# A two-layer hybrid encoder step: up-projection of the gated feed-forward by seven block products per tile pair, down-projection as a phase of its own

## The reference, cut to what matters

```
def conv_ffn(h, w_in, conv_w, conv_b, w_out, pad):
    T = h.shape[1]
    u = h @ w_in                      # 1024 -> 2 * 2816
    up = jnp.concatenate([pad.astype(u.dtype), u], axis=1)
    c = conv_b + sum(up[:, j:j + T] * conv_w[j] for j in range(CONV_W))
    g, val = jnp.split(c, 2, axis=-1)
    y = (jax.nn.silu(g) * val) @ w_out
    return y, up[:, up.shape[1] - (CONV_W - 1):]
```

## Time and profile before

| | |
|---|---|
| median of three runs | 3229.93 us (3226.78 to 3233.74) |
| profiled execution | span 3231.0 us from first to last instruction; of its own time no other figure is given |
| TensorE, matmuls | 3061.2 us busy, 95% of the span |
| VectorE | 2022.1 us, 63% |
| ScalarE | 1139.7 us, 35% |
| GpSimd | 984.7 us, 30% |
| granted TensorE clock, mean | 0.983 of full |
| first feed-forward | about 702 to 1490 us of the span |
| second feed-forward | about 2251 to 3039 us |

### The profile page before, as it was taken

The page is one execution under the profiler, slowest core; times in us unless marked ns, Lnnn a source line. Parts: engine busy times, 40 slices in busy tenths (PEclk is TensorE's granted clock), DMA queues, the critical chain, the costliest instruction groups (busy, mean ns, idle before and its releaser), DMA issues.

```text
span 3231.0 us, 50014 instructions
## 1 busy us (share of the span) xinstructions
PE 3061.2 (95%) x18949; PEld 2945.9 (91%) x18949; DVE 2022.1 (63%) x3233; ACT 1139.7 (35%) x2398; POOL 984.7 (30%) x591
## 2 busy tenths in 40 slices
PE   7999999899999999998987999999999999999998
PEld 6888888799999999998977888889999999999997
DVE  6666666347666556667776677762766666555765
ACT  4555555223221222223340666651322222222243
POOL 2222222222222212222324677753222221222231
PEclk9999999899999999999988999999999999999999
DMA  5222222311111111111104121221111111111111
GB/s 114 70 69 72 67 68 89 106 40 43 44 46 46 42 44 45 41 45 55 40 25 125 31 59 51 83 94 46 40 46 47 46 40 46 46 40 46 55 40 62
DMA packets 255742, 181.94 MB, mean 56 GB/s; under 512 B 26981, under 2 KB 238645, under 8 KB 255541
## 3 DMA queue, kind: packets, MB, share of 16 engines
q1 hardware_dynamic: 240728, 165.11, 17.9%
q10 hardware_dynamic: 14812, 13.97, 1.4%
HBM read 142.54 MB, written 36.50 MB: 55 GB/s over the span
## 4 chain that ended last, share of the span: by engine, by line
PE 76%; DVE 11%; issue 6%; ACT 5%; POOL 1%; DMA 1%; ACTq 0%; DVEq 0%; SPq 0%; POOLq 0%
PE ps L963 22%; PE ps L965 21%; PE ps L964 21%; PE ps L1146 2%; ACT t L1662 2%; PE ps L1281 2%; PE ps L1099 2%; PE ps L1082 2%; PE ps L1166 1%; DVE t L2170 1%; DVE t L2093 1%; DVE ps L2085 1%; DVE t L2020 1%; ACT t L1718 1%; PE ps L1261 1%
## 5 line engine op out<-in xcount | busy, mean ns | idle before, releaser
L963 PE MATMUL ps<-t,t 128*128 128x384 f32 (+1 forms) x4920 | 1648.7, 335 | 52.7 <-issue 10.6
L965 PE MATMUL ps<-t,t 128*128 128x384 f32 (+1 forms) x4920 | 1616.1, 328 | 0.0
L964 PE MATMUL ps<-t,t 128*128 128x384 f32 (+1 forms) x4920 | 1614.5, 328 | 0.0
L963 PEld LDWEIGHTS ps<-t,t 128*128 128x128 f32 x4920 | 931.4, 189 | 91.0 <-issue 24.1
L964 PEld LDWEIGHTS ps<-t,t 128*128 128x128 f32 x4920 | 932.1, 189 | 1.2 <-issue 0.5
L965 PEld LDWEIGHTS ps<-t,t 128*128 128x128 f32 x4920 | 930.7, 189 | 0.0
L780 POOL TENSOR_TENSOR t<-t,t 128x1024 fp32r<-128x1024 f32 x181 | 471.2, 2603 | 1238.9 <-ACT t L1549 1235.5
L1979 DVE TENSOR_TENSOR t<-t,ps 128x384 f32<-128x384 f32 x528 | 260.0, 523 | 147.1 <-PE ps L965 145.0
L1549 ACT ACTIVATE t<-t 128x1024 fp32r<-128x1024 f32 x130 | 138.0, 1061 | 413.8 <-PE ps L965 413.8
L2265 DVE TENSOR_SCALAR t<-t 128x2 f32 (+1 forms) x88 | 14.7, 167 | 419.7 <-ACT t L1792 419.7
L1780 ACT ACTIVATE t<-ps 128x384 f32<-128x384 f32 x176 | 86.4, 494 | 470.1 <-PE ps L965 470.1
(11 more groups left out here) (168 smaller groups left out, 3316.3 us busy)
## 6 DMA issues: line engine op xcount, KB each, us to landing
t<-in_w_ffn_in SPq DMA_DIRECT2D x88, 512.0 KB, 3.7
t<-in_w_ffn_out SPq DMA_DIRECT2D x44, 512.0 KB, 3.2
t<-in_w_qkv_a SPq DMA_DIRECT2D x24, 512.0 KB, 3.8
t<-in_w_ple_gate SPq DMA_DIRECT2D x16, 512.0 KB, 3.5
out<-t SPq DMA_DIRECT2D x32, 192.0 KB, 2.1
t<-in_w_o_a SPq DMA_DIRECT2D x8, 512.0 KB, 3.7
t<-in_w_q_b SPq DMA_DIRECT2D x8, 512.0 KB, 4.2
t<-in_w_o_b SPq DMA_DIRECT2D x8, 512.0 KB, 3.7
```

What stands on the lines that cost most here:

```text
L963: pe.matmul(out, a_hi, b_hi, start=start, stop=False, skip_group_check=True)
L964: pe.matmul(out, a_hi, b_lo, start=False, stop=False, skip_group_check=True)
L965: return pe.matmul(out, a_lo, b_hi, start=False, stop=stop, skip_group_check=True)
```

## The change: what it does, and the diff

The first two tile pairs of a layer are made as before. The other 20 (PAIRS) take block products. The up-projection of a pair is seen as a 2 x 2 block product. A11 and A12 are the gate tile's weights for the first and the second half of k (4 k-tiles x 128 outputs each), A21 and A22 the value tile's. The activations are the two halves of k by the first two segments. Seven products of 4 k-tiles at 384 columns replace eight; the third segment of 320 columns stays a plain product of four blocks.

- Weights: SP loads the four blocks (256 KB each) of the next pair as soon as the product that used the old block is done (blk_done 1, 3, 6, 8). GpSimd makes S1 to S4 from them (four instructions of 512 columns) and the rest of all eight (`block_rest`); ScalarE rounds all eight. Each of the eight has one slot.
- Activations: three combined operands t_hi/t_lo (4 k-tiles x 384) and a fourth, kept in DRAM and then laid over the first half of h's second segment (t4). They are made once per layer at its entry: VectorE makes four parts of 384 columns for each of four k-tiles from x (`combined_parts`), GpSimd combines them (`combine`, four instructions for each k-tile), ScalarE rounds, and VectorE subtracts (`combined_low`).
- Sums: ScalarE copies the first product out; VectorE makes five sums of 384 columns, each with one input from PSUM (u2, u3, and three into ubuf). TensorE accumulates A12's product on the first bank, and S4's on the bank of S1 once VectorE has read it (sums_made 3).
- Filter and gate have the same instructions as before, in the order of `pair` and `gate_half` on VectorE.
- A gated tile (ffr, 557 KB) goes to DRAM (`store_tile`). When the pairs are done the tiles come back four at a time (`load_tiles`), are rounded by ScalarE into h_hi and subtracted by VectorE into h_lo (`tile_high`, `tile_low`).
- Down-projection: six blocks, five of four tiles and one of two, 24 jobs each; a job sums over 4 k-tiles. There are 144 adds per layer instead of 264, in eight banks (JOB_BANKS), in the last block five.

The core of the diff (indentation of 12 columns taken off where a line has it; "..." marks what is left out):

```diff
+PAIRS = NFF - 2
+F_ADDS = 6
+F_CHUNKS, F_JOBS = 4 + 4 * 5 + 2, 8 + 4 * 5 * 5 + 22
+U_KEPT = 12 + 3 * PAIRS
+JOB_BANKS = (7, 1, 2, 4, 6, 5, 0, 3)
+LAST_BANKS = (7, 4, 6, 5, 3)
...
+    def load_block(name, n):
+        q, k0 = divmod("A11 A12 A21 A22".split().index(name), 2)
+        n0 = DFF * q + P * (2 + n)
+        sp.dma_start(slots[l][name][2].rearrange("p (k n) -> p k n", n=P),
+                     w_ffn_in[l].rearrange("(k p) n -> p k n", p=P)[:, 4 * k0:4 * k0 + 4, n0:n0 + P]
+                     ).then_inc(blk_loaded[name], 16)
+    def store_tile(t):
+        sp.wait_ge(ff_made, f0 + t + 1)
+        sp.dma_start(ff_dram[:, t, :], ffr[:, 0:T]).then_inc(ff_stored, 16)
+    def load_tiles(j):
+        for k in range(4 if j < 5 else 2):
+            sp.dma_start(ff_raw[j % 2][:, k, :], ff_dram[:, 4 * j + k, :]).then_inc(ff_loaded[j % 2][k], 16)
+    def down_chunk(j, h):
+        c = c0 + 4 + 4 * j + h
+        if j < 5:
+            load_chunk(c, 0, 0, w_raw[c % 2][:, :].rearrange("p (k n) -> p k n", n=256),
+                       w_ffn_out[l].rearrange("(k p) n -> p k n", p=P)[:, 4 * j:4 * j + 4, 256 * h:256 * h + 256])
...
+    sp.wait_ge(chunk_done, c0 + 3)
+    load_block("A11", 0)
+    load_block("A21", 0)
+    sp.wait_ge(comb_made, COMB_MADE + 16 * (l + 1))
+    load_block("A22", 0)
...
+    sp.wait_ge(chunk_done, c0 + 4)
+    load_block("A12", 0)
+    for n in range(PAIRS):
+        done = 8 * (PAIRS * l + n)
+        if n < PAIRS - 1:
+            sp.wait_ge(blk_done, BLK_DONE + done + 1)
+            load_block("A11", n + 1)
+            sp.wait_ge(blk_done, BLK_DONE + done + 3)
+            load_block("A21", n + 1)
+            store_tile(n + 1)
+            sp.wait_ge(blk_done, BLK_DONE + done + 6)
+            load_block("A22", n + 1)
+            sp.wait_ge(blk_done, BLK_DONE + done + 8)
+            load_block("A12", n + 1)
+        else:
+            sp.wait_ge(blk_done, BLK_DONE + done + 1)
+            down_chunk(0, 0)
+            store_tile(n + 1)
+            sp.wait_ge(blk_done, BLK_DONE + done + 5)
+            down_chunk(0, 1)
...
+def combine(l, k):
+    made = 16 * l + 4 * k
+    h11, h12, h21, h22 = parts[k % 2]
+    pool.wait_ge(comb_hn, COMB_HN + 4 * l + k + 1)
+    pool.tensor_tensor(t_raw[0][:, k, :], h12, h11, ALU.subtract).then_inc(comb_made, 1)
+    pool.tensor_tensor(t_raw[2][:, k, :], h22, h12, ALU.subtract).then_inc(comb_made, 1)
+    pool.wait_ge(comb_made, COMB_MADE + made + 1)
+    pool.tensor_tensor(t_raw[1][:, k, :], h22, t_raw[0][:, k, :], ALU.subtract).then_inc(comb_made, 1)
+    pool.wait_ge(comb_made, COMB_MADE + made + 3)
+    if k:
+        pool.wait_ge(comb_stored, COMB_STORED + 128 * l + 32 * k)
+    pool.tensor_tensor(t4_raw, h21, t_raw[1][:, k, :], ALU.subtract).then_inc(comb_made, 1)
...
+    def block_rest(name, high):
+        hi, lo, raw = S[name]
+        pool.wait_ge(blk_high, BLK_HIGH + 8 * m + high)
+        pool.tensor_tensor(lo, raw, hi.bitcast(F32), ALU.subtract).then_inc(blk_split, 1)
+    pool.wait_ge(blk_loaded["A11"], BLK_LOADED + 16 * (m + 1))
+    pool.wait_ge(blk_loaded["A21"], BLK_LOADED + 16 * (m + 1))
+    if n:
+        pool.wait_ge(blk_done, BLK_DONE + 8 * (m - 1) + 2)
+    else:
+        pool.wait_ge(chunk_done, c0 + 3)
+    pool.tensor_tensor(S["S3"][2], S["A11"][2], S["A21"][2], ALU.subtract).then_inc(s_made, 1)
+    pool.wait_ge(s_made, S_MADE + 4 * m + 1)
+    block_rest("A11", 1)
+    pool.wait_ge(blk_loaded["A22"], BLK_LOADED + 16 * (m + 1))
+    if n:
+        pool.wait_ge(blk_done, BLK_DONE + 8 * (m - 1) + 4)
+    pool.tensor_tensor(S["S2"][2], S["A22"][2], S["S3"][2], ALU.subtract).then_inc(s_made, 1)
+    if n:
+        pool.wait_ge(blk_done, BLK_DONE + 8 * (m - 1) + 5)
+    else:
+        pool.wait_ge(w_split, c0 + 4)
+    pool.tensor_tensor(S["S1"][2], S["A21"][2], S["A22"][2], ALU.add).then_inc(s_made, 1)
+    pool.wait_ge(s_made, S_MADE + 4 * m + 3)
+    block_rest("S3", 3)
+    block_rest("A21", 2)
+    pool.wait_ge(blk_loaded["A12"], BLK_LOADED + 16 * (m + 1))
+    if n:
+        pool.wait_ge(blk_done, BLK_DONE + 8 * (m - 1) + 7)
+    else:
+        pool.wait_ge(chunk_done, c0 + 4)
+    pool.tensor_tensor(S["S4"][2], S["A12"][2], S["S2"][2], ALU.subtract).then_inc(s_made, 1)
+    pool.wait_ge(s_made, S_MADE + 4 * m + 4)
+    block_rest("S2", 5)
+    block_rest("S1", 6)
+    block_rest("A22", 4)
+    block_rest("S4", 8)
+    block_rest("A12", 7)
...
+    c0 = at[f"F{l}"][0]
+    split(c0 + 1, ffn=l)
+    combine(l, 0)
+    combine(l, 1)
+    split(c0 + 2, ffn=l)
+    combine(l, 2)
+    combine(l, 3)
+    split(c0 + 3, ffn=l)
+    for n in range(PAIRS):
+        pair_weights(l, n)
+    last = 8 * (PAIRS * (l + 1) - 1)
+    pool.wait_ge(blk_done, BLK_DONE + last + 2)
+    split(c0 + 4, ffn=l)
+    pool.wait_ge(blk_done, BLK_DONE + last + 8)
+    split(c0 + 5, ffn=l)
+    splits(c0 + 6, c0 + f_chunks, l)
...
+    def pair(n):
+        m, kept = PAIRS * l + n, u0 + 12 + 3 * (n - 1)
+        pe.wait_ge(blk_split, BLK_SPLIT + 8 * m + 1)
+        pe.wait_ge(u_kept, kept + 2 if n else u0 + 10)
+        product(0, "A11", h_first[:, :, 0:384], l_first[:, :, 0:384], True).then_inc(part_done, 1)
+        if n:
+            pe.wait_ge(u_kept, kept + 3)
+        product(5, "A11", h_first[:, :, 768:T], l_first[:, :, 768:T], True).then_inc(blk_done, 1)
+        pe.wait_ge(blk_split, BLK_SPLIT + 8 * m + 2)
+        if n:
+            pe.wait_ge(sums_made, SUMS_MADE + 5 * (m - 1) + 2)
+        else:
+            pe.wait_ge(u_kept, u0 + 12)
+            pe.wait_ge(comb_low, COMB_LOW + 16 * (l + 1))
+        product(2, "S3", t_hi[2], t_lo[2], True).then_inc(blk_done, 1)
+        pe.wait_ge(blk_split, BLK_SPLIT + 8 * m + 3)
+        product(6, "A21", h_first[:, :, 768:T], l_first[:, :, 768:T], True).then_inc(blk_done, 1)
+        pe.wait_ge(blk_split, BLK_SPLIT + 8 * m + 4)
+        product(1, "S2", t_hi[1], t_lo[1], True).then_inc(blk_done, 1)
+        pe.wait_ge(blk_split, BLK_SPLIT + 8 * m + 5)
+        if n:
+            pe.wait_ge(sums_made, SUMS_MADE + 5 * (m - 1) + 5)
+        product(3, "S1", t_hi[0], t_lo[0], True).then_inc(blk_done, 1)
+        pe.wait_ge(blk_split, BLK_SPLIT + 8 * m + 6)
+        if n == 0:
+            pe.wait_ge(t4_loaded, T4_LOADED + 32 * (l + 1))
+        product(4, "A22", h_first[:, :, 384:768], l_first[:, :, 384:768], True)
+        product(6, "A22", h_second[:, :, 768:T], l_second[:, :, 768:T], False).then_inc(blk_done, 1)
+        pe.wait_ge(blk_split, BLK_SPLIT + 8 * m + 7)
+        pe.wait_ge(sums_made, SUMS_MADE + 5 * m + 3)
+        product(3, "S4", h_second[:, :, 384:768], l_second[:, :, 384:768], False).then_inc(blk_done, 1)
+        pe.wait_ge(blk_split, BLK_SPLIT + 8 * m + 8)
+        pe.wait_ge(p1_kept, P1_KEPT + m + 1)
+        product(0, "A12", h_second[:, :, 0:384], l_second[:, :, 0:384], False).then_inc(part_done, 1)
+        product(5, "A12", h_second[:, :, 768:T], l_second[:, :, 768:T], False).then_inc(blk_done, 1)
...
-    down(c0 + 64, 0, (0, 10), 0)
+    for n in range(PAIRS):
+        pair(n)
+    for j in range(6):
+        down(j)
     pe.wait_ge(tail_set, 2 * NU * (l + 1))
-    pe.wait_ge(u_kept, 3 * NU * (l + 1))
+    pe.wait_ge(u_kept, U_KEPT * (l + 1))
     for kind in range(2):
         pe.transpose(ps[0:88, kind, 0:P], tail[:, 88 * kind:88 * kind + 88], ident[:, :]).then_inc(tail_turned, 1)
...
+    def pair(n):
+        m, unit = PAIRS * l + n, u0 + 4 + 2 * n
+        more = n < PAIRS - 1
+        act.wait_ge(part_done, PART_DONE + 2 * m + 1)
+        if m:
+            act.wait_ge(sums_made, SUMS_MADE + 5 * (m - 1) + 1)
+        act.activation(p1_sum, ps[:, 0, 0:384], ACT.Copy).then_inc(p1_kept, 1)
+        loaded_high("A12", n)
+        made_high("S4", n, 4)
+        if more:
...
+        if n:
+            sigmoid(n + 1, unit - 1)
+        if more:
+            loaded_high("A21", n + 1)
+            made_high("S3", n + 1, 1)
+        act.wait_ge(blk_done, BLK_DONE + 8 * m + 6)
+        act.wait_ge(conv_step, 3 * (unit - 1) if n else 3 * unit)
+        last_segment(ubuf[1], 6)
+        if more:
+            loaded_high("A22", n + 1)
+        else:
+            for k in range(4):
+                tile_high(0, k)
+        act.wait_ge(part_done, PART_DONE + 2 * m + 2)
+        act.wait_ge(conv_step, 3 * unit)
+        act.activation(ubuf[0][:, 2:386], ps[:, 0, 0:384], ACT.Copy).then_inc(u_kept, 1)
+        if more:
+            made_high("S2", n + 1, 2)
+        act.wait_ge(blk_done, BLK_DONE + 8 * m + 8)
+        last_segment(ubuf[0], 5)
+        if more:
+            made_high("S1", n + 1, 3)
+    kept(0, 0)
+    combined_high(0)
+    kept(0, 1)
+    combined_high(1)
+    kept(0, 2)
...
+    kept(1, 0)
+    combined_high(2)
+    kept(1, 1)
+    combined_high(3)
+    sigmoid(0, u0)
+    kept(1, 2)
+    weights_high(c0 + 3, 0)
+    for s in range(3):
+        kept(2, s)
+    kept(3, 0)
+    loaded_high("A11", 0)
+    loaded_high("A21", 0)
+    made_high("S3", 0, 1)
...
```

(33 more changed lines are left out.)

424 lines of the change are left out of this document (277 added, 147 removed).

## The result

The changed kernel takes 3254.28 us, the kernel before 3231.15 us, each the median of four runs. One of the changed kernel's four, of 3315.72 us, ran in a slower state with a granted clock of 0.88 and is left out of the ratio; the other three have a median of 3252.62 us. The ratio is 1.0064, with a 95% interval of 1.005 to 1.0078: slower, by about 20 us. The forecast was slower by 76. The profiled execution has a span of 3247.0 us, 16.0 more than before.

What follows compares the result with a forecast made beforehand. The prediction took GpSimd's and VectorE's shared SBUF work to bound the pairs, above TensorE's 21.56 us. Per layer 27 + 16 + 2 - 7 = +38, two layers +76: 3307 us, 3306 against the median; range 3190 to 3400.

Steps and rivals of the forecast that it cites:

- the saving of work: TensorE's matmuls in one pair: 21.56 us, 2.09 less than 23.65; 83 us over 40 pairs if TensorE stays the bound.
- the turns: GpSimd and VectorE alternate on a pair's SBUF work; a turn costs 0.27 us less than the sum of its records.
- the walk of three pairs: Pairs followed step by step: S4 starts 24.6, 25.7, 24.3 us apart; 25.0 taken per pair, +27 us per layer.
- the plain count of turns: One pair: 26.1 us of GpSimd's and VectorE's SBUF work less 3.2 for twelve turns, 22.9 us, the lower end.
- a sign of being wrong: In the pairs: a pair released by a GpSimd rest or a load instead of VectorE's third sum.
- the entry: Each layer's start: TensorE waits 11 us for the third chunk, 2.5 for the fourth, some half clock; +16 us.
- the change of phase: Pairs to down-projection: loading and splitting four tiles takes 24 us against a pair of 25; +2 us per layer.
- the gain at the end: Each layer's end: the 4.8 us wait for the last tile's rest and 2.2 us of half clock go; -7 us.
- A: Rival, pairs: TensorE stays the bound, locked work under 21.56 us; -31 us per layer, 3169 us; chance 0.16.
- B: Rival, pairs: full exclusion, a turn costs both records whole, 26.7 us per pair; 3375 us; chance 0.2.
- C: Rival, clock: waits of 3 to 4 us per pair at S4 bring half clock; 3375 us; chance 0.12.
- D: Rival, loads: A12 and A22 land after 4 us instead of 3, S2's rest late; up to +1 per pair, 3347.

Runs made afterwards that it cites:

- experiment 1: Changed kernel with the second and third filter step on 64 instead of 1090 columns, most of the convolution left out: 3203.29 us in one run.
- Experiment 2: Changed kernel with SP issuing the next A22 load one product later, after S4: 3270.02 us in one run.
- experiment 5: Run block_order: changed kernel, A22's group ahead of S2 and S1, A12's first part ahead of S4: 3271.86 us, ratio 1.012 to the kernel before.
- experiment 6: Run t4_raw: changed kernel, t4 sent to DRAM unsplit from two buffers and split once when back: 3254.78 us, ratio 1.0067 to the kernel before.
- experiment 10: Run a21_vector: experiment 7's kernel, second tile's gate product behind the first pair's sums, A21's rest on VectorE from the second pair: 3230.27 us, ratio 0.9997.
- Experiment 4: Run entry_order: changed kernel, entry reordered, third and fourth chunk ahead of most combinations, first sigmoid later: 3262.99 us, ratio 1.0099 to the kernel before.
- experiment 7: Changed kernel with the edits of Experiment 4 and experiment 6 together: 3237.98 us, ratio 1.0032 to the kernel before.
- Experiment 8: Changed kernel with the second group of four tiles loaded after the two following chunks of weights: 3252.53 us, ratio 1.0068 to the kernel before.
- experiment 3: Kernel before with the feed-forward's five-fold loops written out on all engines, same work and order: 3226.38 us, ratio 0.998 to the kernel before.
- experiment 11: Experiment 7's kernel, second tile's gate product behind the first pair's sums, S2's rest on VectorE from the second pair: 3241.12 us, ratio 1.0026.

## Why the prediction had the sign and missed the size

**Right: the sign, the saving of work and the turns.** The matmuls of a pair were put at 21.56 us: in experiment 1, with VectorE's load lightened, TensorE was never short of work for long, and the pair took 22.0. The filter steps are held by GpSimd's instructions (the third step has a mean of 2216 ns, 1350 alone), and a turn costs less than the sum of its records: 0.27 us less by the earlier trace rows, 0.29 to 0.37 here. The five sums with PSUM stayed at 0.54 to 0.56 us beside GpSimd, as assumed. By the Trainium skill (SBUF — State Buffer, "SBUF: two separate sides") the loser of the shared port pair blocks until the other's end. Its figure of about 115 ns more is from a DMA whose descriptors GpSimd can't write while VectorE copies; the prediction carried it over to these turns. The blocking agrees with these rows, the addition does not, for a turn is shorter than the sum and not longer.

**Wrong, and most of the miss: the walk of three pairs**, which gave 24.6, 25.7 and 24.3 us with TensorE 3 to 4 us short of the third sum, and the choice of 25.0 from it. The pair is 23.1, close to the lower end of 22.9 that the plain count of turns had given. In the trace TensorE would reach S4 some 15.8 us into its pair, as the walk had it, but the third sum is there at 16.6 (1017.65, for a pair that starts at 1001.09) and not 3 to 4 us late. S2's rest comes at 9.0 us, due at 7.7; the forecast had given it a slack of 2 us. This is the release by a GpSimd rest that the prediction had named as a sign of being wrong. What the walk overlooked is in part argued: it had put the two engines' work in a chain, and the trace shows that each works while the other waits. VectorE's steps of 0.83 and 1.35 us run whole while GpSimd waits 1.6 us for A22's block, and GpSimd's run whole at 1.29 to 1.30 while VectorE makes its sums and waits for TensorE (0.86) and for ScalarE (0.38). Experiment 2 shows it by force: 1.5 of a delay of 2.08 us were absorbed in that way. Both rings are near 23 us, GpSimd's through S2's rest and VectorE's through the third sum; experiments 5, 6 and 10 let the second take over at once, and the prediction had the wrong one in front. This term was +27 per layer and is -11, 38 too much. That the total came out no further off is luck, for the other terms partly hid it: the entry was 13 too low, the change of phase 6 too low, the gain at the end 11 too small; 38 - 13 - 6 + 11 = 30 per layer is the whole miss.

**Too low: the entry**, +16 against +29. The third chunk was nearly right: its split was forecast for 751.5 and ends at 752.8, and TensorE waits 13.8 us instead of 11, though the turns are shorter (1.3 us) and a wait of 3.4 us for t4's buffer was left out. The step that failed is the 2.5 us for the fourth chunk, put in without a count of what stands ahead of it; it was 12.3. Ahead of it stand eight more combinations from 752.8 to 768.5, held up by the first filter (up to 2.07 us each beside its steps) and by the second wait for t4's buffer (4.3), and then a sigmoid that waits for the last store and loads a table (3.9 + 1.3 us). Experiment 4 shows that its order is not enough, experiment 6 that a shorter way for t4 is not enough, and experiment 7 that the two edits together gain 11 to 15 us; which of their parts are needed stays open, as said there.

**Too low: the change of phase**, +2 against +8. The forecast had the loads issued 11.8 us into the last pair, landed after 10, and 2.4 for copy and rest: 24.2 us under a pair of 25. The last pair starts at 1232.3, and the loads are issued 15.7 us later: S1 ends at some 1245.6, since S2 had waited, and on SP the store of a gated tile stands ahead, which VectorE finishes at 1247.2. The last copy starts 11.2 us after the issue, and the pair is over after 23.3. Of a store ahead of A22's load the forecast had spoken, of this one not. Experiment 8 rules out the second group of tiles as the cause. Whether loads ahead of that store would help was not tried.

**Too small: the gain at the end**, -7 against -18. The named term is right: the wait of 4.78 us and its half clock are gone, 7 us. Not seen were the turns of the loops, which experiment 3 puts at 3 us per layer, and ten small waits for the adds. Each of these shows as 0.23 us idle but costs 0.5 by the starts of the matmuls: at 1043.76 the next starts after 0.57 us instead of 0.17, and the one behind it after 0.25 instead of 0.15. That is 5 us per layer. Of the 3 us that are left some 2 lie in the stretch before: over the whole layer the matmuls of 384 columns start every 0.1745 us and not 0.173, so 20 pairs took 475 us and not 473.

**The rivals.** A, TensorE as the bound, needed less shared work; only experiment 1 came near it, with 22.0 us. B is refuted by the turn of 2.35 us. C's condition did not come: the waits of each pair are 1.16 us, and the clock stays at full through the pairs (1.00 in the window from 794 to 1255). What waits of 3 to 4 us per pair would have cost is not shown. At 4.3 us and more the clock was at its lower level behind every wait of TensorE's in the feed-forwards of these runs, but between 2 and 4 us both are found, as the last section shows. D named the right place, S2's rest, though the loads were not late.

## What to carry to other kernels

Saving TensorE's work pays only to the next ring: here 2.09 us less per pair became 0.5, because GpSimd's and VectorE's rings, tied together by their turns, both stood at 23 us, and moving work between them (experiments 5, 10, 11) moved the wait. Estimate such a pair first by the sum of shared work less a bit per turn, and let each engine work in the other's waits; a chain walked overstates it. And count the one-off parts, buffers that wait for a store and rounding queued behind a sigmoid among them: over two layers the entry took back 59 us, more than the 22 that the pairs gave.

## What the runs showed of the hardware that was not expected

- A late GpSimd makes itself up: with 2.2 us more idle time its two next instructions took 1.29 us each instead of 1.86 and 2.35.
- Small operations are held as well: in run a21_vector a step of 2 columns took 1.19 us beside GpSimd, and 0.17 to 0.27 when alone. Its row:

```profile
994.96 1.19 DVE L2643 TENSOR_SCALAR t<-t 128x2 f32<-128x2 f32 x1 [0.90 <-ACT t L2039]
```

- The length of a wait alone does not say whether the clock falls behind it. In run t4_raw TensorE waited 2.45 us for the third sum up to 856.45 and went on at full clock; in run block_order it waited 2.18 us up to 860.46 and went on at a mean of 0.65; behind a wait of 2.47 us in run a21_vector it was 0.50, and behind one of 3.58 us in run entry_order (2353.58) 1.00. The windows of the first two:

```profile
856.40:859.40 3.00, 2.95 (x17) 2.98 (x18) 2.82 (x7) 0.59 (x1) 0.55 (x1) 1.00 0.55 152
...
860.50:863.50 3.00, 3.00 (x12) 3.00 (x13) 2.89 (x5) 0.00 (x0) 3.00 (x3) 0.65 0.09 36
```

- Of two edits of the entry one changed nothing by itself, the other cost 10 us by itself, and together they gained 11 to 15 us.
